# PEER experts of a four-stage block: one gather holds two picks of 64 tokens, the products are 128x64 side by side, rows are normed ahead of the dots

## What is computed

```python
def _rmsnorm(x, g):
    xf = x.astype(jnp.float32)
    xf = xf * lax.rsqrt(jnp.mean(xf * xf, axis=-1, keepdims=True) + EPS)
    return xf.astype(x.dtype) * g

def one_chunk(xt):                       # xt: 128 tokens, already _rmsnorm(h, norm2_g)
    q = (xt @ w_q).reshape(BLOCK, PEER_HEADS, PEER_QDIM)            # 8 heads of 256
    s1 = jnp.einsum('chd,nd->chn', q[..., :half], keys1)            # 128 keys each
    s2 = jnp.einsum('chd,nd->chn', q[..., half:], keys2)
    t1, i1 = lax.top_k(s1, PEER_TOPK)                               # 16 of 128, twice
    t2, i2 = lax.top_k(s2, PEER_TOPK)
    cand = (t1[..., :, None] + t2[..., None, :]).reshape(...)       # 256 sums
    cidx = (i1[..., :, None] * PEER_NKEYS + i2[..., None, :]).reshape(...)
    ts, sel = lax.top_k(cand, PEER_TOPK)                            # 16 of 256
    idx = jnp.take_along_axis(cidx, sel, axis=-1)
    g = jax.nn.softmax(ts, axis=-1)
    act = jax.nn.gelu(jnp.einsum('chkd,cd->chk', u[idx], xt))       # a dot with a row of u
    coef = g * act
    return jnp.einsum('chk,chkd->cd', coef, v[idx])                 # a sum of rows of v

h = h + _peer(_rmsnorm(h, norm2_g[l]), ...)
h = _rmsnorm(h, final_g)                 # and the first 16 tokens are dropped
```

## Time and profile before

| | |
|---|---|
| median of three runs | 1424.19 us (1422.96 to 1424.39) |
| span of the profiled execution | 1418.2 us, so 6.0 us of the median lie around a span like it |
| TensorE (matmul) busy | 1290.9 us, 91% |
| VectorE busy | 900.7 us, 64% |
| ScalarE busy | 424.8 us, 30% |
| GpSimd busy | 290.9 us, 21% |
| DMA | 414.87 MB, mean 293 GB/s |
| DMA queue of the gathers | 269.50 MB |
| chain that ended last | PE 52%, DMA 25%, DVE 7% |
| mean granted TensorE clock | 0.989 |

### The profile page before, as it was taken

How to read it: one execution, slowest core, us unless ns; L and a number is a source line. 1 busy time by engine, 2 the same in 40 slices (tenths; PEclk the granted TensorE clock), 3 DMA queues, 4 the chain that set the end, 5 groups by cost and what they waited for, 6 DMA issues and landing times.

```text
span 1418.2 us, 22747 instructions
## 1 busy us (share of the span) xinstructions
PE 1290.9 (91%) x8590; PEld 879.1 (62%) x8590; DVE 900.7 (64%) x2446; ACT 424.8 (30%) x1140; POOL 290.9 (21%) x269
## 2 busy tenths in 40 slices
PE   7999998999999999998999899998788788887776
PEld 3446788986579898997776556775344344333222
DVE  7527876546564463147585677556777778778755
ACT  1215223121351153013333374113222322222223
POOL 0000000000000000010222333323464344444440
PEclk9999999999999999999999999999999999999999
DMA  8444100343324675889999999999999999999995
GB/s 314 157 154 135 33 4 3 119 148 119 119 90 167 218 271 182 275 289 377 394 422 386 421 362 388 421 421 418 425 425 424 423 424 425 425 425 424 425 425 222
DMA packets 82957, 414.87 MB, mean 293 GB/s; under 512 B 10847, under 2 KB 15327, under 8 KB 49761
## 3 DMA queue, kind: packets, MB, share of 16 engines
q0 software_dynamic: 37152, 269.50, 45.9%
q1 hardware_dynamic: 45554, 143.66, 28.5%
q10 hardware_dynamic: 144, 0.26, 0.0%
HBM read 412.33 MB, written 1.06 MB: 291 GB/s over the span
## 4 chain that ended last, share of the span: by engine, by line
PE 52%; DMA 25%; DVE 7%; issue 2%; ACT 2%; POOL 1%; DVEq 0%; SPq 0%; POOLq 0%; ACTq 0%
DMA arena<-peer_in,arena 20%; PE bank L1890 13%; PE bank L2886 12%; PE bank L1422 3%; DMA row<-peer_in,arena 2%; DMA ring<-stream_in 2%; PE bank L2792 2%; PE bank L1502 2%; PE bank L1479 2%; PE bank L843 2%; DVE arena L3142 2%; PE bank L2078 2%; PE bank L652 1%; PE bank L642 1%; PE bank L1554 1%
## 5 line engine op out<-in xcount | busy, mean ns | idle before, releaser
L2886 PE MATMUL bank<-arena 128*128 128x512 f32 x812 | 385.9, 613 | 66.7 <-ACT arena L2995 66.4
L3191 POOL DMA_INDIRECT arena<-peer_in,arena x203 | 225.6, 1112 | 526.3 <-PE bank L2886 353.7
L3142 DVE CUSTOM_DVE_ANT_0 arena<-arena 128x1024 f32<-128x1024 f32 x203 | 247.9, 1225 | 108.3 <-DMA arena<-peer_in,arena 104.3
L2886 PEld LDWEIGHTS bank<-arena 128*128 128x128 f32 x812 | 148.2, 195 | 247.9 <-issue 247.8
L1890 PEld LDWEIGHTS bank<-arena,ring 128*128 128x128 f32 x1984 | 232.1, 192 | 24.7 <-issue 21.6
L1890 PE MATMUL bank<-arena,ring 128*128 128x128 f32 (+1 forms) x1984 | 236.3, 277 | 5.7 <-DMA ring<-stream_in 4.1
L2986 ACT ACTIVATE arena<-arena 128x2 f32<-128x2 f32 (+1 forms) x130 | 38.3, 295 | 319.6 <-DVE arena L3142 319.4
L2995 ACT ACTIVATE arena<-cst,arena 128x128 f32<-128x128 f32 x256 | 90.9, 394 | 48.4 <-DVE arena L3081 44.4
L2662 POOL COPY arena<-wide 64x1152 f32<-64x1152 f32 x2 | 2.3, 1140 | 351.1 <-DVE wide L2416 351.0
L2792 PEld LDWEIGHTS bank<-arena,ring 128*128 128x128 f32 x512 | 62.9, 196 | 14.9 <-issue 11.5
L2792 PE MATMUL bank<-arena,ring 128*128 128x128 f32 x512 | 63.8, 280 | 2.1 <-DVE arena L2553 2.1
(11 more groups left out here) (397 smaller groups left out, 1814.9 us busy)
## 6 DMA issues: line engine op xcount, KB each, us to landing
ring<-stream_in SPq DMA_DIRECT2D x243, 512.0 KB
ring<-stream_in SPq DMA_DIRECT2D x16, 384.0 KB
arena<-peer_in,arena POOLq DMA_INDIRECT x203
row<-rows_in SPq DMA_DIRECT2D x4, 512.0 KB, 17.6
ring<-stream_in SPq DMA_DIRECT2D x16, 128.0 KB
cst<-cst_in SPq DMA_DIRECT2D x1, 1868.0 KB, 18.2
row<-rows_in POOLq DMA_DIRECT2D x2, 512.0 KB, 6.1
cst<-rg_w_in SPq DMA_DIRECT2D x1, 1024.0 KB, 7.6
```

The source lines that it names most:

```text
L2886: mm = nc.tensor.matmul(core.banks[2 * t + b][:, :], diag[i % ND], places[seat[i]][:, D + b * 512:D + (b + 1) * 512], start=False, stop=last)
L3142: ins = nc.vector.tensor_tensor_reduce(out=row, in0=row, in1=X2[t], scale=1.0, scalar=0.0, op0=ALU.mult, op1=ALU.add, accum_out=dots[:, i: ...
L3191: pool.indirect_dma_start(out=places[seat[i]], out_offset=None, in_=g.names["peer"], in_offset=bass.IndirectOffsetOnAxis(ap=index[:, i:i + ...
```

## The change

A gather now holds two picks of 64 tokens instead of one pick of 128. Of picks 2q and 2q+1, the first gather takes both for tokens 0 to 63 (pick 2q on partitions 0 to 63, pick 2q+1 on partitions 64 to 127), the second gather both for tokens 64 to 127. The number of gathers and their bytes stay.

- The diagonal becomes 128x64: two identities of 64, one above the other (`halves`), scaled by row. Its product with the v half of a seat is 64 tokens by 512, summed over both picks, and goes to partitions 0 to 63 of the bank (first gather) or 64 to 127 (second). TensorE issues the four products of a pair together, after waiting for both landings and both diagonals; before, it waited for each pick apart. So both calls of `advance` now stand ahead of the four products.
- `X2[t]` becomes two tiles: tokens 0 to 63 repeated on both halves of the partitions, and tokens 64 to 127 repeated. `turn_twice` makes them with 32 products of 128x64 against the identity, where `turn` had eight transposes, and `keep_twice` copies them out in four pieces, scaled by `rstd`. `bend`, `steep` and `half_rstd` go, and the scales of the gelu are constants.
- At the start of the stage the rows of R (`turn("x")`) are turned and copied ahead of the first scores, the rows of `X2` after the scores of unit 1, and `scale(0)` stands inside the first `route`. For half 1 the same order holds within the steps spread among the picks.
- `index`, `weight` and the scale of the rows are written in four pieces of 64 partitions, since they change places between the halves.
- The arena grows by 512 floats, X2 takes two tiles more, and the later seats number 5 instead of 6: 12 in all, before 13.

```diff
+    ("ones", P), ("halves", HP2), ...
+    put("halves", np.concatenate([np.eye(HP2), np.eye(HP2)], 0))
...
-    X2, R = [plan("x2"), plan("share")], plan("r")
+    X2 = [[plan("x2", 0, D), plan("x2", D, D)], [plan("share"), plan("zb", PLAN["zb"][1] - D, D)]]
-    late_at, late_n = PLAN["k2"][0], (PLAN["seats"][0] - PLAN["k2"][0]) // ROW
+    late_at, late_n = PLAN["k2"][0], (PLAN["seats"][0] - D - PLAN["k2"][0]) // ROW
+    def rows_of(b):
+        return slice(b * HP2, (b + 1) * HP2)
+    CORNERS = [(j, a) for j in range(2) for a in range(2)]
... TensorE
+        def turn_twice(t, j):
+            for quad in range(2):
+                key = ("twice", t, j, quad)
+                bank = claim(pe, key)
+                for i in range(4):
+                    for a in range(2):
+                        mm = nc.tensor.matmul(bank[rows_of(a), i * P:(i + 1) * P], n2[t][:, 4 * quad + i, rows_of(j)], cst("ident"),
+                                              start=True, stop=True)
...
-                for k in (2 * q, 2 * q + 1):
-                    i = n * TOPK + k
-                    advance(i + SKEW["pe"])
-                    for b in range(2):
-                        if b == 0:
-                            pe.wait_ge(landed[seat[i]].handle, 16 * (turn_no[i] + 1))
-                            pe.wait_ge(diag_ready.handle, i + 1)
-                        mm = nc.tensor.matmul(core.banks[2 * t + b][:, :], diag[i % ND], places[seat[i]][:, D + b * 512:D + (b + 1) * 512],
-                                              start=False, stop=last)
-                    mm.then_inc(*used.up())
+                for i in (pair, pair + 1):
+                    advance(i + SKEW["pe"])
+                def weighted_row(i, b):
+                    j = i - pair
+                    return nc.tensor.matmul(core.banks[2 * t + b][rows_of(j), :], diag[i % ND],
+                                            places[seat[i]][:, D + b * 512:D + (b + 1) * 512], start=False, stop=last)
+                for i in (pair, pair + 1):
+                    pe.wait_ge(landed[seat[i]].handle, 16 * (turn_no[i] + 1))
+                pe.wait_ge(diag_ready.handle, pair + 2)
+                for i in (pair, pair + 1):
+                    mm = weighted_row(i, 0)
+                if last:
+                    mm.then_inc(*half_summed.up())
+                for i in (pair, pair + 1):
+                    weighted_row(i, 1).then_inc(*used.up())
... ScalarE
+        def keep_twice(t, j):
+            act.wait_ge(scale_ready.handle, t + 1)
+            for b in range(2):
+                nc.scalar.activation(half(X2[t][j], b), bank[:, :], ACT.Copy, scale=by_row[:, 2 * t + j:2 * t + j + 1])
-                        nc.scalar.activation(diag[i % ND], cst("ident"), ACT.Copy, scale=act_out[:, i:i + 1])\
+                        nc.scalar.activation(diag[i % ND], cst("halves"), ACT.Copy, scale=act_out[:, i:i + 1])\
... VectorE
-            nc.vector.scalar_tensor_tensor(out=unit(index, n), in0=lead, scalar=float(NK), in1=index_f, op0=ALU.mult,
-                                           op1=ALU.add).then_inc(*routed.up())
+            for j, a in CORNERS:
+                ins = nc.vector.scalar_tensor_tensor(out=unit(index, n)[rows_of(a), j::2], in0=lead[rows_of(j), a::2], scalar=float(NK),
+                                                     in1=index_f[rows_of(j), a::2], op0=ALU.mult, op1=ALU.add)
+            ins.then_inc(*routed.up())
-                        ins = nc.vector.tensor_tensor_reduce(out=row, in0=row, in1=X2[t], scale=1.0, scalar=0.0,
+                        ins = nc.vector.tensor_tensor_reduce(out=row, in0=row, in1=X2[t][i % 2], scale=1.0, scalar=0.0,
```

More of the change, by code:

```diff
@@ L42 @@
 RING = 8
+HP2 = 64
+ARENA = 16 * 2048 + 512
 WIDE = (NM + P, P)
@@ L2705, in experts @@
     index_f, lead = carve(TOPK), carve(TOPK)
-    chosen = carve(N * TOPK)
+    best = carve(TOPK)
+    shares = carve(N * TOPK)
     index = carve(N * TOPK).bitcast(U32)
@@ L2817, in turn @@
                 g.at[key] = g.now
+        def turn_twice(t, j):
[6 more added lines that the diff above has]
+                                              start=True, stop=True)
+                mm.then_inc(*full(key))
+                g.at[key] = g.now
         def begin_sum(t):
@@ L2835, in front @@
             scores(HP)
-            turn("n2", n2[1], 1)
+            yield ("score", HP), 3
+            for j in range(2):
+                turn_twice(1, j)
+                yield 0.5
         steps = front()
@@ L2862, in _ @@
         query(0, 1)
-        turn("n2", n2[0], 0)
+        turn("x", x[:, :, 0:P], 0)
         pe.wait_ge(keys_loaded.handle, 16)
         scores(0)
[L2866 to L2870, removed]
+        query(1, 0)
+        query(1, 1)
+        scores(1)
+        for j in range(2):
+            turn_twice(0, j)
+        query(2, 0)
+        query(2, 1)
+        scores(2)
         core.rotation, core.next_bank = [4, 5, 6, 7], 0
@@ L2914, in turn @@
                 nc.scalar.activation(half(dst, b), bank[:, :], ACT.Copy).then_inc(*free(key))
+        def keep_twice(t, j):
+            act.wait_ge(scale_ready.handle, t + 1)
+            for b in range(2):
+                key = ("twice", t, j, b)
+                bank = filled(act, key)
+                nc.scalar.activation(half(X2[t][j], b), bank[:, :], ACT.Copy, scale=by_row[:, 2 * t + j:2 * t + j + 1])\
+                  .then_inc(*free(key))
         def root(t):
             copied(act, ("turn", "x", t, 1))
-            spare = X2[1] if t else diag_flat
-            nc.scalar.activation(spare, R, ACT.Square, accum_out=rstd[:, t:t + 1]).then_inc(*squared.up())
+            nc.scalar.activation(X2[t][0], R, ACT.Square, accum_out=rstd[:, t:t + 1]).then_inc(*squared.up())
             act.wait_ge(squared.handle, t + 1)
@@ L2928, in exps @@
             act.wait_ge(scale_ready.handle, t + 1)
-            nc.scalar.activation(unit(weight, n), unit(weight, n), ACT.Exp, scale=rstd[:, t:t + 1],
+            nc.scalar.activation(unit(shares, n), unit(shares, n), ACT.Exp, scale=rstd[:, t:t + 1],
                                  accum_out=total[:, n:n + 1]).then_inc(*exped.up())
@@ L2964, in front @@
             scores(HP)
-            yield ("turn", "n2", 1, 1), 2
-            turn("n2", X2[1], 1)
+            for j in range(2):
+                yield ("twice", 1, j, 1), 2
+                keep_twice(1, j)
         advance = paced(front(), SKEW["act"])
         query(0)
+        turn("x", R, 0)
         scores(0)
-        turn("n2", X2[0], 0)
-        turn("x", R, 0)
         root(0)
-        for n in (1, 2):
-            query(n)
-            scores(n)
+        query(1)
+        scores(1)
+        for j in range(2):
+            keep_twice(0, j)
+        query(2)
+        scores(2)
         for i in range(START, 0):
@@ L3119, in front @@
             yield from g.later["dve"]
-            yield ("turn", "x", 1, 1), 4
+            yield ("turn", "x", 1, 1), 3
             scale(1)
         advance = paced(front(), SKEW["dve"])
-        for _ in route(0):
+        first = route(0)
+        for _ in range(6):
+            next(first)
+        scale(0)
+        for _ in first:
             pass
-        scale(0)
         second = route(1)
```

61 lines of the change are left out of this document (31 added, 30 removed).

## The result

The changed kernel takes 1433.78 us (1432.68 to 1435.43, four runs), the kernel before 1423.58 us: a ratio of 1.007, 95% interval 1.0056 to 1.0085. It is 10.2 us slower, where 6 us faster was forecast. The profiled execution after has a span of 1433.6 us and a device time of 1435.43 us, so only 1.8 us lie around a span. With as much around it, the profiled execution before (span 1418.2 us) took about 1420.0 us: it was a quick one, and the 6.0 us that the prediction puts around a span are mostly that. The spans differ by 15.4 us, the medians by 10.2: spans show here where time went, medians how much.

The account below looks back on a forecast made before the run. DMA transfers were taken as the bound, with TensorE nearly level from 660 to 980 us. Span 1418.2 - 9 (transfer time regained) + 2.0 (start) + 0.5 = 1411.7 us, plus 6.0 around it, say 1418 us; range 1408 to 1428.

Parts of the forecast that it names:

- the 6.0 us that the prediction puts around a span: Whole kernel: 6.0 us lie around the span of before, 1424.19 against 1418.2 us, and are added to the forecast span.
- The products: Pairs on TensorE: halves run at once, so a pair's products take 1.72 us instead of 3.44, about 1.98 with shape changes.
- the small price forecast: TensorE between steps and pairs: both changes of array shape together cost 0.26 us, no danger to the 1.72 us saving.
- The start: Stage start: first gather leaves 1 to 1.7 us later, turn_twice frees no ring slot for 2.4 us more; 2.0 us together.
- The last part: From 980 us on: DMA alone sets the pace and stays at 424 GB/s as before; 0.5 us added for the end.
- rival 5: From 980 us on: the clock stays at 1.2 GHz, adding 3 us and 1 us at the end, 1422 us; chance 0.05.
- The step that failed: 660 to 680 us: of 3.5 us of lost transfer time, 1 us comes back, with bounds of 0 and 3.5.
- the term of 9 us: 660 to 980 us: 9 of 17.4 us of lost transfer time come back, with DMA at 410 to 415 GB/s.
- Rival 3: 640 to 980 us: pairs hold scarce seats too long, 0.3 us per pair over 43 pairs, 13 us, 1431 us; chance 0.12.
- Rival 4: Products of the pairs: the halves don't overlap at 512 columns in one bank, 14 us slower, 1438 us; chance 0.03.
- rival 2: 660 to 980 us: all 17.4 us of lost transfer time come back, 1409.3 us; chance 0.13.
- Rival 1: 660 to 980 us: lost transfer time is not TensorE's, nothing comes back, 1426.7 us; chance 0.15.

Follow-up runs that it names:

- e11: e5 with the 32 products of turn_twice of half 0 and their copies moved behind the third query and its scores: 1417.94 us, ratio 0.9968.
- e1: The kernel before with both advances and both landing waits of a pair ahead of its four unhalved products on TensorE: 1440.88 us, ratio 1.0121.
- e14: The kernel before, without pairs, with TensorE's steps of the second mixer 4 picks ahead of the products instead of 3: 1440.1 us, ratio 1.0112.
- e2: The changed kernel with the second advance of a pair behind the pair's four products instead of ahead of them: 1419.02 us, ratio 0.9961.
- e16: e5 with 6 seats instead of 7 from pick 12 to 111: 1433.96 us, ratio 1.0074.
- e5: e2 with both diagonals of a pair also made together on ScalarE, the mixer step between them moved behind both: 1418.73 us, ratio 0.9972.
- e8: e5 with both steps of the mixer behind the pair's products on TensorE: 1419.59 us, ratio 0.9969.
- e10: The changed kernel with both mixer steps of a pair ahead of both dots on VectorE, TensorE's order unchanged: 1435.6 us, ratio 1.0088.
- e15: The kernel before with TensorE's steps of the second mixer 2 picks ahead of the products instead of 3: 1418.53 us, ratio 0.9976.
- e7: The kernel before in pairs, as e1, but with the second mixer step behind the four 128x128 products: 1424.3 us, ratio 1.0004.
- e6: e2 with both products of one column half ordered before both of the other: 1420.67 us, ratio 0.9979.

## Why the prediction was wrong

What bounds the kernel was read rightly: transfers set the time, and TensorE's saving counts only where it lets DMA run.

- *The products.* Right. 671.25 to 673.12 us after is 1.87 us for a pair with its change of shape; 1.98 was forecast. TensorE's 1175.9 us busy are more than the 1100 forecast: the clock fell. A record of the products takes 1.06 us at 854.28 us, where the granted clock was 0.74 (840 to 860 us), against a median of 0.59 over the mixed part. For the drain of a change of mode (the Trainium skill, TensorEngine Tiling, Key Properties) 1.87 against 1.72 us leaves 0.15 us, so the small price forecast held.
- *The start.* Right in kind: 16.0 us from the first query to the first gather before (613.61 to 629.60), 17.5 after (615.82 to 633.3), 1.5 us more; 1 to 1.7 was forecast. The absolute time ("after 632 us") could not tell: in the six traces that start like the kernel before, the first gather leaves between 629.6 and 633.2 us. What the whole start costs is not settled: e11 moved the DMA and not the time.
- *The last part.* From 1100 us on the clock was 0.78, and DMA ran at 425: rival 5's low clock was there in part and cost nothing. From 980 to 1100 us DMA had 409 GB/s against 424 before, 4 us that the forecast had at nothing ("424 from 980 us on as before"). e1 (408) and e14 (413) have such a hole without the new rows of half 1, so it isn't theirs alone; its cause is open. The end was not slowed, 1426.49 to 1427.77 us from the last pair's first product to the closing square, 1.28 us against 1.27.
- *The step that failed* is the one at 660 to 680 us: "After the change two steps stand ahead of the first pair, not one, and both seats come free together, about where the mean of the two was." With it went the 9 us of transfer time that should have come back, and the mixed part lost 9 us more instead. The step counted the second step ahead of the pair as 1.79 us of TensorE's time, which one seat loses and the other wins back. It left out what that step itself waits for: a part on ScalarE or VectorE that stands behind the dots of later gathers. At 680 us that held two landed seats for 16 us. e2 shows the price, 14.8 us for the place of one step; e1 and e14 show it again on the kernel before, 18 and 17.5 us. e16 shows that seats are scarce.
- *With the order mended* the term of 9 us holds: e2, e5 and e8 have 408, 412 and 410 GB/s from 660 to 980 us, where 410 to 415 was forecast, 7 to 10 us of transfer time over 399. Only 4 to 5 us of that reach the time. From 980 to 1100 us e2 and e5 still have 413 and 415 GB/s, about 3 us less than before, and the start takes the 1.5 us above.
- *Rival 3* named scarce seats behind two steps, the place and 0.3 us per pair, and forecast 1431 us. Measured against e2 the changed kernel loses 14.8/43 = 0.34 us per pair. That the mean fits so well is in part luck, since the loss comes in two places and not pair by pair. The rival got a chance of 0.12 on the argument just quoted; its other argument, that the seats were busy until the pair's coefficients came, was no excuse either: of some 40 pairs from 640 to 980 us, TensorE waited for a diagonal in only 5.
- *Rival 4* falls by the products and *rival 2* by the sign. *Rival 1* (nothing comes back, 1426.7 us) falls by the 387 GB/s, where it had 399, and by e5's 412.
- *A row misread.* "From slice 23 on the core moves 418 to 425 GB/s" is true from the 26th slice of the earlier trace rows on; 362 and 388 stand just ahead of it. The sum did not use it.

What stays open: the waiting steps are read from the traces at 680 and 840 us, but no run takes the waits away and leaves the order. e10 tried it for VectorE alone, without gain. And e5, e11 and e15 all end near 1418 us: the side-by-side products are worth 5 us in one order (e7 to e2), but a change of one number on the kernel before (e15) gets 4 us of it without them.

## What to carry to other kernels

Where a fixed order mixes work that frees a scarce buffer with work that doesn't, put the freeing work first. Of each instruction that stands ahead of it, ask what that one waits for, and not only how long it takes; a mean over two buffers hides it. Before valuing a faster engine by the transfer time that it could give back, shift its instructions by one place and see what that alone costs. TensorE was busy for 115 us less, and the halved products were worth 5 us; one place in its queue was worth 15.

## What the runs showed of the hardware

Products for the two column halves of the array ran at once also where they did not alternate in the program (e6), with four whole products in a pair. From 980 to 1400 us, with TensorE busy for 263 of 420 us and idle ahead of pairs (6.37 us at 1021.84), the granted clock fell to a mean of 0.78, in stretches at 1.2 GHz: the records of a pair then start 0.85 us apart in each half and not 0.43. TensorE's rows after, of one seat of a pair:

```profile
1022.72 1.06 PE L2914 MATMUL bank<-cst,arena 128*64 128x512 f32 x1
...
1023.57 1.06 PE L2914 MATMUL bank<-cst,arena 128*64 128x512 f32 x1
```
